# Other banks for scores and values, a later mean, and a new order of decay, keys and bonus in two mixers

## The reference, cut to what matters

```python
z = xn @ w_in[l]
z_rw = z_rw + shift_mu[l] * (_time_shift(z_rw) - z_rw)
r, k, v, xw, xa, xg = _split_cols(z_rw, RW_SPLITS)
if l == 0: v_first = v
else:      v = v + (v_first - v) * sigmoid(vres_bias + (xn @ vres_down) @ vres_up)
# RWKV: decay = exp(-exp(w_log)), kk = normalized k * k_k, k = k * (1 + (a - 1) * k_a)
y = _rwkv7_recurrence(r, decay, k, v, kk, kk * a)
bonus = sum(r * k * r_k, over a head) * v
y_a = (_head_standardize(y) * gn_w + gn_b + bonus) * g
# mLSTM: qk = silu(causal conv of q and k), scores * exp(gaps), causal, then sums over tokens
h = numerator / max(|denominator|, exp(-m));  y_b = sigmoid(mo) * _head_standardize(h) * norm_w
u = sigmoid(g_a) * (y_a @ br_a[l]) + sigmoid(g_b) * (y_b @ br_b[l])
h = h + u @ w_out[l]
```

## Time and profile before

| | us |
|---|---|
| median of 3 runs | 2405.29 (2403.14 to 2405.49) |
| profiled execution | 2402.39 |
| its span on the core | 2400.6 |
| TensorE busy | 2311.4 (96%) |
| VectorE busy | 1752.7 (73%) |
| ScalarE busy | 1275.5 (53%) |

### The profile page before, as it was taken

How to read it: one execution, slowest core, us unless ns; L and a number is a source line. 1 busy time by engine, 2 the same in 40 slices (tenths; PEclk the granted TensorE clock), 3 DMA queues, 4 the chain that set the end, 5 groups by cost and what they waited for, 6 DMA issues and landing times.

```text
span 2400.6 us, 44999 instructions
## 1 busy us (share of the span) xinstructions
PE 2311.4 (96%) x16696; PEld 2049.0 (85%) x16696; DVE 1752.7 (73%) x2779; ACT 1275.5 (53%) x1942; POOL 27.5 (1%) x66
## 2 busy tenths in 40 slices
PE   7999999999999999999999999999999999999998
PEld 7888978888888768888889898888888888888887
DVE  6888988888988677767667575766666676747666
ACT  5445454454445565446446562654554475536444
POOL 0000000000000000000000000000000000000000
PEclk9999999999999999999999999999999999999999
DMA  9886978868997316655555441455555543415553
GB/s 328 276 294 235 357 262 293 289 222 285 327 316 263 106 54 209 225 199 165 189 188 176 131 148 37 161 190 187 189 177 187 191 165 127 147 33 170 195 192 123
DMA packets 130438, 480.67 MB, mean 200 GB/s; under 512 B 14608, under 2 KB 14784, under 8 KB 129776
## 3 DMA queue, kind: packets, MB, share of 16 engines
q1 hardware_dynamic: 128448, 467.62, 57.7%
q0 software_dynamic: 1840, 10.93, 1.2%
HBM read 477.41 MB, written 1.07 MB: 199 GB/s over the span
## 4 chain that ended last, share of the span: by engine, by line
PE 77%; DVE 10%; ACT 6%; issue 4%; DMA 2%; SPq 0%; DVEq 0%; ACTq 0%; POOLq 0%; POOL 0%
PE bank L601 75%; ACT work L1413 2%; DMA ring<-weights 2%; DVE w_lo L2071 2%; ACT w_hi L1413 2%; DVE y L2105 2%; PE bank L630 1%; ACT h_split L1413 1%; ACT L1413 1%; DVE y L2261 1%; PE bank L1227 0%; DVE work L2502 0%; DVE y L2634 0%; ACT y L1413 0%; DVE x L2266 0%
## 5 line engine op out<-in xcount | busy, mean ns | idle before, releaser
L601 PE MATMUL bank<-h_split,w_hi 128*128 128x256 f32 (+1 forms) x5344 | 1152.4, 336 | 26.8 <-ACT work L1413 9.3
L2071 DVE TENSOR_TENSOR w_lo<-ring,w_hi 128x1024 fp32r<-128x1024 f32 x715 | 871.2, 1222 | 353.4 <-ACT w_hi L1413 352.3
L1413 ACT ACTIVATE w_hi<-ring 128x1024 fp32r<-128x1024 f32 x726 | 765.8, 1057 | 625.9 <-PE bank L601 533.2
L601 PEld LDWEIGHTS bank<-h_split,w_hi 128*128 128x128 f32 x5344 | 901.5, 191 | 121.3 <-issue 13.8
L601 PE MATMUL bank<-h_split,w_lo 128*128 128x256 f32 x3896 | 754.1, 283 | 0.1
L601 PEld LDWEIGHTS bank<-h_split,w_lo 128*128 128x128 f32 x3896 | 613.6, 191 | 24.4 <-DVE w_lo L2071 0.5
L1413 ACT ACTIVATE work<-bank 128x512 f32<-128x512 f32 (+1 forms) x266 | 154.8, 586 | 327.1 <-PE bank L601 298.5
L601 PE MATMUL bank<-w_hi,act_hi 128*128 128x512 f32 x704 | 275.4, 391 | 0.2
L601 PE MATMUL bank<-w_lo,act_hi 128*128 128x512 f32 x704 | 274.9, 390 | 0.0
L601 PE MATMUL bank<-w_hi,act_lo 128*128 128x512 f32 x704 | 273.9, 389 | 0.0
L2105 DVE CUSTOM_DVE_ANT_0 y<-ring,v_first 128x1024 f32<-128x1024 f32 x160 | 189.4, 1220 | 1.7 <-DMA ring<-weights 1.7
(11 more groups left out here) (226 smaller groups left out, 1569.7 us busy)
## 6 DMA issues: line engine op xcount, KB each, us to landing
ring<-weights SPq DMA_DIRECT2D x886, 512.0 KB, 4.9
work<-cmp POOLq DMA_DIRECT2D x1, 4096.0 KB, 15.1
sq<-rows POOLq DMA_DIRECT2D x6, 512.0 KB, 7.6
work<-lora POOLq DMA_DIRECT2D x2, 1024.0 KB, 5.9
x<-x_in SPq DMA_DIRECT2D x1, 1024.0 KB, 5.7
out<-y SPq DMA_DIRECT2D x2, 512.0 KB, 2.6
const_sb<-consts POOLq DMA_DIRECT2D x1, 726.0 KB, 8.3
v_first<-c_in SPq DMA_DIRECT2D x1, 512.0 KB, 3.6
```

The costliest lines, as they stand in the source:

```text
L601: return nc.tensor.matmul(out, lhsT, rhs, start=start, stop=stop, skip_group_check=skip)
L1413: return nc.scalar.activation(out, in_, f, bias=bias, scale=scale, **kw)
L2071: tt(w_lo[q % SLOTS][:, :], ring[n % RING][:, c * HALF:(c + 1) * HALF], w_hi[q % SLOTS][:, :].bitcast(F32), ALU.subtract).then_inc(halves_ ...
```

## The change

The four scores of `m_scores(0)` go to banks 2 and 3 and wait for `em_copy` instead of `g_col`; those of `m_scores(4)` go to banks 0 and 1 and wait for the last gap instead of `sw3`. `m_sums` waits for the mask of the last score of its own four. `r_w` no longer waits for `sw7`. The values' second half goes to bank 6 and has no front wait. `m_mean` stands after the second half of tile 13. On ScalarE `E` is made before `E_inv`, which is made in place in `e5`, and neither waits for `v_mixed`; `v_hat` is made after `go(45)`. On VectorE the order from `go(35)` on is new, and differs by layer. In the step lists at the head of the kernel the names follow these orders.

```diff
...
@@ -782,17 +782,19 @@
                                       lo3[:, k, :], k == 0, k == KC - 1)
                         ins.then_inc(half_used, 1)
-            def wide(st, t, c, parts):
+            def wide(st, t, c, parts, b=None):
                 f, ts = st.front + t + c, slice(c * P, (c + 1) * P)
-                front_wait(f)
+                if b is None:
+                    front_wait(f)
+                    b = FRONT[f % 2]
                 for i in parts:
                     q = st.half + 2 * t + i
                     half_wait(q)
                     w = q % SLOTS
                     for kk in range(2):
                         k, o = 2 * i + kk, slice(kk * 512, (kk + 1) * 512)
-                        ins = mm3(bank[FRONT[f % 2]][:, :], hi3[:, k, ts], lo3[:, k, ts], w_hi[w][:, o], w_lo[w][:, o],
+                        ins = mm3(bank[b][:, :], hi3[:, k, ts], lo3[:, k, ts], w_hi[w][:, o], w_lo[w][:, o],
                                   k == 0, k == KC - 1)
                     if c:
                         ins.then_inc(half_used, 1)
@@ -1019,22 +1021,21 @@
                     if first == 0:
                         pe.wait_ge(*M.act.at("silu3"))
-                        pe.wait_ge(*M.vec.at("g_col"))
+                        pe.wait_ge(*M.act.at("em_copy"))
                     else:
-                        pe.wait_ge(*M.vec.at("sw3"))
+                        pe.wait_ge(*M.vec.at("gap7"))
                     for i in range(first, first + 4):
                         hd, kt = i // 2, i % 2
-                        mm(half(6 + i % 4 // 2, i % 2)[:, kt * P:TOK], qk[:, 4 + hd, kt * P:(kt + 1) * P],
+                        mm(half((0 if first else 2) + i % 4 // 2, i % 2)[:, kt * P:TOK], qk[:, 4 + hd, kt * P:(kt + 1) * P],
                            qk[:, hd, kt * P:TOK], True, True).then_inc(*M.pe.step(f"scores{i}"))
                 def m_sums(p):
                     b = 2 if p == 0 else 0
-                    pe.wait_ge(*(M.act.at("em_copy") if p == 0 else M.vec.at("gap7")))
+                    pe.wait_ge(*M.vec.at(f"masked{4 * p + 3}"))
                     if p == 0:
                         pe.wait_ge(front_taken, st.front + 7)
                     for hd in (2 * p, 2 * p + 1):
-                        pe.wait_ge(*M.vec.at(f"masked{2 * hd + 1}"))
                         for kt in range(2):
                             mm(half(b, hd % 2)[:, kt * P:TOK], v_tok[:, kt, hd * P:(hd + 1) * P],
                                sw[:, 2 * hd + kt, kt * P:TOK], kt == 0, kt == 1)
@@ -1061,7 +1062,6 @@
                     return ins.then_inc(*R.pe.step(name))
                 def r_w():
-                    pe.wait_ge(*M.vec.at("sw7"))
                     pe.wait_ge(lora_landed, 16 * (l + 1))
                     pe.wait_ge(*R.act.at("lora_w"))
                     low(0, lora_in[:, 0, :], "w")
@@ -1109,9 +1109,9 @@
                 lin_half(st, 4, 0)
                 lin_half(st, 4, 1)
                 wide(st, 5, 0, (0, 1, 2))
-                wide(st, 5, 1, (0, 1, 2))
+                wide(st, 5, 1, (0, 1, 2), SPARE)
                 wide(st, 5, 0, (3,)).then_inc(*M.pe.step("values_0"))
-                wide(st, 5, 1, (3,))
+                wide(st, 5, 1, (3,), SPARE)
                 m_scores(0)
                 lin_half(st, 7, 0)
                 m_scores(4)
@@ -1133,8 +1133,8 @@
                 lin_half(st, 12, 0)
                 lin_half(st, 12, 1)
                 lin_half(st, 13, 0)
+                lin_half(st, 13, 1)
                 m_mean()
-                lin_half(st, 13, 1)
                 lin_half(st, 14, 0)
                 r_kk()
                 lin_half(st, 14, 1)
@@ -1250,8 +1250,8 @@
                         pe.wait_ge(*R.act.at("XK_1"))
                     lin_half(gst, i // 6, i // 3 % 2, ks=FILL_KS[i % 3])
-                pe.wait_ge(*R.vec.at("bhat"))
                 pe.wait_ge(*R.vec.at("bonus1"))
+                pe.wait_ge(*R.vec.at("khat"))
                 pe.wait_ge(front_taken, st.front + 24)
                 first_products(0)
                 first_products(1)
@@ -1728,7 +1728,7 @@
                     else:
                         act.wait_ge(*M.pe.at("values_0"))
                     act.wait_ge(front_taken, n)
-                    fn(v_tok[:, c, :], bank[FRONT[n % 2]][:, :], ACT.Copy).then_inc(front_taken, 1)
+                    fn(v_tok[:, c, :], bank[SPARE if c else FRONT[n % 2]][:, :], ACT.Copy).then_inc(front_taken, 1)
                 def weights(first):
                     for i in range(first, first + 4):
@@ -1848,11 +1848,11 @@
                        ).then_inc(*M.act.step(f"rstd{i}"))
                 go(34)
                 shift_rows(15, 10, 11)
-                go(35 + l)
-                act.wait_ge(*R.vec.at("v_mixed"))
-                fn(e7[:, :, :], e5[:, :, :], ACT.Exp, scale=EXP_MINUS_HALF).then_inc(*R.act.step("E_inv"))
+                go(35)
                 act.wait_ge(*R.pe.at("rk_sum"))
                 fn(e8[:, :, :], e5[:, :, :], ACT.Exp, scale=-EXP_MINUS_HALF).then_inc(*R.act.step("E"))
+                act.wait_ge(*R.act.at("E"))
+                fn(e5[:, :, :], e5[:, :, :], ACT.Exp, scale=EXP_MINUS_HALF).then_inc(*R.act.step("E_inv"))
                 go(36)
                 take(16, u_b[:, 0:2, :], ACT.Sigmoid)
                 act.wait_ge(*M.vec.at("y_b"))
@@ -1863,6 +1863,7 @@
                 take(18, u_b[:, 4:6, :], ACT.Sigmoid)
                 go(42)
                 take(19, u_b[:, 6:8, :], ACT.Sigmoid)
+                go(45)
                 act.wait_ge(*R.vec.at("khat"))
                 for j in range(4):
                     ins = fn(v_hat[:, j // 2, :, j % 2], zp[:, 8 + j].rearrange("p (c t) -> p c t", c=4), ACT.Copy)
@@ -2675,7 +2676,7 @@
                         kt = i % 2
                         dve.wait_ge(*M.act.at(f"weight{i}"))
                         stt(out=sw[:, i, kt * P:TOK], in0=w_buf[:, i, kt * P:TOK], scalar=float(P) ** -0.5,
-                            in1=half(6 + i % 4 // 2, i % 2)[:, kt * P:TOK], op0=ALU.mult, op1=ALU.mult
+                            in1=half((0 if first else 2) + i % 4 // 2, i % 2)[:, kt * P:TOK], op0=ALU.mult, op1=ALU.mult
                             ).then_inc(*Mv.step(f"sw{i}"))
                         dve.wait_ge(*Mv.at(f"sw{i}"))
                         dg = sw[:, i, kt * P:(kt + 1) * P]
@@ -2794,65 +2795,82 @@
                     ins = stt(out=h_b[:, j, :], in0=h_b[:, j, :], scalar=V(f"mlnorm{l}", j), in1=sw[:, j, :],
                               op0=ALU.mult, op1=ALU.mult)
                 ins.then_inc(*Mv.step("normed"))
+                vf = tiles(v_first, 4)
+
+                def by_pairs(t, h):
+                    return t[:, 2 * h:2 * h + 2].rearrange("p e (c t) -> p e c t", c=4)
+
+                def in_pairs(t, h):
+                    return t[:, h].rearrange("p c e t -> p e c t")
+
+                def bonuses():
+                    for i in range(2):
+                        tt(bonus[:, 2 * i:2 * i + 2, :], pair(2 + i), zp[:, 8 + 2 * i:10 + 2 * i, :], ALU.mult
+                           ).then_inc(*Rv.step(f"bonus{i}"))
+
+                def b_hat():
+                    dve.wait_ge(*R.act.at("E_inv"))
+                    dve.wait_ge(*Rv.at("kap"))
+                    for h in range(2):
+                        ins = tt(in_pairs(bhat, h), by_pairs(e4, h), by_pairs(e5, h), ALU.mult)
+                    ins.then_inc(*Rv.step("bhat"))
+
+                def k_hat():
+                    for h in range(2):
+                        ins = tt(in_pairs(khat, h), by_pairs(zk, h), by_pairs(e5, h), ALU.mult)
+                    ins.then_inc(*Rv.step("khat"))
+
                 go(35)
-                vf = tiles(v_first, 4)
-                dve.wait_ge(front_taken, st.front + 16)
...
-                go(36)
                 dve.wait_ge(*Mv.at("normed"))
                 dve.wait_ge(*M.act.at("sig_o1"))
                 tt(y_b[:, :, :], h_b[:, :, :], m_o[:, :, :], ALU.mult).then_inc(*Mv.step("y_b"))
+                go(36)
                 dve.wait_ge(*Rv.at("kk"))
                 tt(e4[:, :, :], e4[:, :, :], e3[:, :, :], ALU.mult).then_inc(*Rv.step("b"))
-                go(37)
                 dve.wait_ge(*R.act.at("E_prev"))
                 tt(kap[:, :, :], e3[:, :, :], e6[:, :, :], ALU.mult).then_inc(*Rv.step("kap"))
+                go(37)
                 dve.wait_ge(*M.act.at("yb_hi"))
                 for i in range(2):
                     o = slice(2 * i, 2 * i + 2)
                     ins = tt(y_lo[i], y_b[:, o, :], y_hi[:, o, :].bitcast(F32), ALU.subtract)
                 ins.then_inc(*Mv.step("yb_lo"))
-                go(38)
...
-                go(39)
                 dve.wait_ge(*R.act.at("E"))
                 tt(rho[:, :, :], zr, e8[:, :, :], ALU.mult).then_inc(*Rv.step("rho"))
+                go(38)
                 pcol = small[:, 20:36].rearrange("p (e h c) -> p e h c", e=2, h=2)
```

(63 more changed lines are left out.)

9 lines of the change are left out of this document (removed).

## The result

The changed kernel's median is 2382.26 us (2381.26 to 2383.84, 4 runs), the kernel before's 2404.22 us (2402.86 to 2405.49, 4 runs). The ratio is 0.9906, with a 95% interval from 0.9894 to 0.9918. Measured again later, the same pair gave 2383.06 and 2404.20 us (5 and 9 runs), ratio 0.9913 (0.9900 to 0.9927). The gain is 21 to 22 us. The direction was as forecast, and every wait that the forecast named is gone; 2387.0 us was too slow by 4.7 us, and 2382.26 lies 0.7 us under the low end of the range. Of the 4.7 us, 1.1 is the kernel before's own median (2405.29 us when the forecast was made, 2404.22 here) and 3.7 is gain that was not forecast.

What follows compares the result with a forecast made beforehand. TensorE's matmuls, busy 96% of the span, were taken as the bound; 6.54 + 1.39 + 1.34 + 2.90 + 5.67 + 0.85 - 0.4 = 18.3 us saved gave 2387.0 us, range 2383 to 2393.5.

Steps and rivals of the forecast that it cites:

- Restarts: Between half tiles on TensorE: each removed wait also saves 0.08 us, eleven waits, 0.85 us in all.
- clock: Layer 0, second scores to first sums: the slow stretch behind the score stall goes, 1.39 us.
- case E: Granted clock on TensorE: slow stretches behind both score stalls give 2385.6 us, one more met 2388.4; chance 0.12, either sign.
- Part 1: Score products in free banks: the wait of 3.27 us before the second four goes in both layers, 6.54 us.
- Part 2: Value projection's second half in the spare bank: its wait on VectorE's convolution goes, 0.67 us a layer, 1.34 in all.
- Part 3: Means' sum a half tile later: its wait on VectorE's head outputs goes in both layers, 2.90 us.
- Part 4: New order of decay, keys and bonus: waits before tile 18 and on weight splits go, 5.67 us.
- Give-back: At `first_products`, waiting for VectorE's last branch multiply: 0.4 us lost for both layers, bounds 0 and 2.
- rival B: VectorE becomes the bound of the mixer's last stretch, exposing moved pairs and the copy: 2392.6 us; chance 0.12.
- C: The score wait comes back at the sums or weight splits, plus a mean wait: 2391.8 us; chance 0.08.
- D: Tile 18's wait stays because something other than the exponentials held ScalarE's take: 2391.2 us; chance 0.04.
- F: Weight stream: TensorE outruns the transfers and waits at each of 88 halves, 2414 us at 160 GB/s; chance 0.03.

## Why the prediction was wrong

The failed term is **Restarts**: 0.85 us in the sum, 2.6 us measured. I had taken the unstalled half tile as 2.965 us, from four halves that ended at an idle time. The printed idle time starts when the last matmul's row ends, 0.28 us after its start, though the next could have started after 0.12. So those four halves already held the drain of the stall behind them: 11.86 us, where four halves without it take 11.61. Eight halves without any wait take 23.22 us, 2.90 each. Against that, the stage of layer 0 lost 2.83 us for 2.10 us printed and that of layer 1 4.31 for 3.57, 0.24 and 0.37 us a wait. Over both mixers, with slow clock left out, the gain is 18.5 us. The idle times removed are the 16.45 us of the prediction, less the new 0.50. The other 2.6 us belong to eleven waits gone less two new ones, 0.29 each.

The second term that was sized too low is the **clock**, 1.39 us. The profile that I had showed a slow stretch in one layer. Seven of eight layers with this stall have one, filling the stall gained 2.9 us, and the runs' granted clocks give about 3. I also had no term for the stall before tile 18, 3.13 us in layer 1, which has a slow stretch behind it in three of four profiles. How the 3 us divide between the two stalls stays open. My case E named the score stalls' part (2385.6 us, a chance of 0.12 for either sign), but beside A and not in it.

Point by point. **Part 1** right in its mechanism: no wait at the sums, none on the masks; the stage shrank to 11.24 us where I asked for 7.2 between second scores and sums (7.07). **Part 2** right. **Part 3**: `r_kk` does not wait for `centred`, as worked out, but I never asked whether half 27 was split when TensorE comes to it earlier, by the 1.45 us of the wait and the 1.54 us of the mean's own products that used to lie in front. It was not, by 0.25 us, 0.5 with the drain, in each layer. The stage gained 1.2 us instead of 1.45 and a restart. **Part 4** right in its sum of idle times and wrong in its shares: I gave tile 18's wait to ScalarE in both layers and the split waits to VectorE's order in both. In layer 0 ScalarE's order removes all of them. In layer 1 it leaves waits for splits of 2.08 us in place of 3.57, unless VectorE's order changes too. **Give-back**: 0.4 us predicted, 0.06 in layer 0 and nothing in layer 1. VectorE's timeline at the end of layer 1 after shows how it kept up, its last split ending just ahead of the last multiply:

```profile
2072.66 1.21 DVE L2072 TENSOR_TENSOR w_lo<-ring,w_hi 128x1024 fp32r<-128x1024 f32 x1
2074.01 0.69 DVE L2877 TENSOR_TENSOR work<-work,bank 128x512 f32<-128x512 f32 x1
```

That, and the 0.06 us, speak against rival B. C fell with the scores' stage, D with ScalarE's row at 1402.07. F fell with the time itself, and TensorE's waits after the change name no transfer.

The **range** had a slip too. Its high end is said to take B, C and 1.4 us of clock; added to 2387.0 these give 2398.8 us, not 2393.5. Its low end, 2383, allowed only a little more for the restarts, and these needed 1.7 us more.

The sum with the measured sizes: 18.5 us, and 2.9 for the clock, make 21.4, against 21.1 and 22.0 measured. Against the forecast's 18.3 us, the restarts brought 1.7 us more, the clock 1.5, the give-back 0.3, and the new waits took 0.5. What stays open is how often a stall sets off a slow stretch, and for how long; the profiles show seven of eight for idle times of 3.27 us, and one of them twice as long.

## What to carry to other kernels

Price a removed TensorE wait at its printed idle time plus the drain and refill, 0.24 to 0.37 us here, and get the unstalled rate from a stretch with no wait at either end; better still, compare the starts of whole stages. A stall of a few microseconds has a second price in the clock, which one profile may not show. A stretch that one stall no longer sets off can turn up behind the next, so count them over several profiles. Where the stall can't go, matmuls that nobody reads are worth their room. When TensorE is moved earlier, ask for every weight half on its new path whether it will be there, also where the moved step itself has slack.

## What the runs showed of the hardware that was not expected

A wait for nothing but TensorE's own last matmul costs 0.37 us between two streams of 256-column matmuls, of which 0.15 us is idle time between rows (2.57 us for seven). The lower clock level after one and the same stall of 3.27 us lasted once about twice as long as otherwise (a stage of 17.53 us against 16.2 to 16.4). An idle time of 1.89 us was enough for a stretch in five of eight layers (0.79 over 8 us behind it). And 28 matmul instructions in each mixer whose result is dropped made the kernel before faster by 2.9 us (1 to 6).
